# Routed experts' weights in a fused decoder kernel: one transfer of two chunks as 128 runs of 8 KB instead of 256 runs of 4 KB

## The reference

```python
def swiglu(x, w1, w3, w2):
    return (jax.nn.silu(x @ w1) * (x @ w3)) @ w2

def moe(h, w_router, router_bias, w1, w3, w2, ws1, ws3, ws2):   # E = 64, D = 1024, F = 256
    t = h.reshape(-1, D)                                        # 512 tokens
    scores = jax.nn.sigmoid((t @ w_router).astype(jnp.float32))
    _, eidx = lax.top_k(scores + router_bias.astype(jnp.float32), TOP_K_EXPERTS)
    ...
    def expert_block(args):                                     # 128 rows of one expert
        e, toks, gs = args
        xb = t[toks]
        return swiglu(xb, w1[e], w3[e], w2[e]) * gs[:, None]
    out = lax.map(expert_block, ...)
    routed = jax.ops.segment_sum(out.reshape(rows, D), row_tok, num_segments=n_tok)
    shared = swiglu(t, ws1, ws3, ws2)
    return (routed + shared).reshape(B, S, D)
```

## Time and profile before

| | us |
|---|---|
| median of 3 runs | 2543.27 |
| lowest and highest | 2539.15, 2545.02 |
| the profiled execution | 2526.87 |
| its span, first to last instruction | 2525.1 |

### The profile page before, as it was taken

One profiled execution on the slowest core, in us unless ns is written; L12 is line 12 of the kernel. 1 busy time (PEld: TensorE's weight loads), 2 busy tenths in 40 slices (PEclk: granted clock), 3 DMA queues, 4 the chain that ended last, 5 costly groups with the idle time before them and its releaser, 6 DMA issues.

```text
span 2525.1 us, 31999 instructions
## 1 busy us (share of the span) xinstructions
PE 2293.0 (91%) x10228; PEld 1778.9 (70%) x10228; DVE 1562.7 (62%) x2400; ACT 1195.4 (47%) x1778; POOL 283.9 (11%) x345
## 2 busy tenths in 40 slices
PE   6998999599999999994598989999989888999997
PEld 4776677487777777773475778887768556888875
DVE  6789654698888888886674553333453566433334
ACT  4432433298888888884235332233231673322322
POOL 0000002423223322324200000000000000000000
PEclk8999997799999999998699999999999989999999
DMA  7521132599999999996420222223313101232232
GB/s 305 200 95 64 42 130 94 150 357 380 371 365 368 372 355 357 359 339 238 175 93 8 67 75 100 91 100 100 100 67 100 34 1 67 100 100 93 99 101 83
DMA packets 124602, 422.63 MB, mean 167 GB/s; under 512 B 21024, under 2 KB 21152, under 8 KB 124384
## 3 DMA queue, kind: packets, MB, share of 16 engines
q1 hardware_dynamic: 98176, 367.86, 41.1%
q0 software_dynamic: 25376, 50.66, 5.3%
q10 hardware_dynamic: 960, 2.97, 0.3%
HBM read 419.68 MB, written 39.47 MB: 182 GB/s over the span
## 4 chain that ended last, share of the span: by engine, by line
PE 60%; DMA 16%; DVE 13%; issue 5%; ACT 4%; DVEq 1%; SPq 0%; POOL 0%; ACTq 0%; POOLq 0%
PE PS L283 17%; PE PS L285 17%; PE PS L284 17%; DMA eraw<-wstream 14%; DVE wl L191 3%; PE PS L628 3%; PE PS L650 2%; ACT wh L186 2%; DVE YA L2308 1%; PE PS L639 1%; DMA ada_w<-wada 1%; DVEq L1188 1%; ACT YS L1902 1%; DVE M L1185 1%; DVE X L555 1%
## 5 line engine op out<-in xcount | busy, mean ns | idle before, releaser
L191 DVE TENSOR_TENSOR wl<-raw,wh 128x1024 fp32r<-128x1024 f32 x239 | 292.5, 1225 | 403.3 <-ACT wh L186 396.9
L283 PE MATMUL PS<-HTh,wh 128*128 128x512 f32 x1248 | 503.8, 404 | 39.5 <-DVE HTl L581 18.7
L191 DVE TENSOR_TENSOR wl<-eraw,wh 128x1024 fp32r<-128x1024 f32 x384 | 460.1, 1225 | 73.5 <-ACT wh L186 72.9
L284 PE MATMUL PS<-HTl,wh 128*128 128x512 f32 x1248 | 492.0, 394 | 0.0
L285 PE MATMUL PS<-HTh,wl 128*128 128x512 f32 x1248 | 491.6, 394 | 0.0
L186 ACT ACTIVATE wh<-eraw 128x1024 fp32r<-128x1024 f32 x384 | 392.4, 1054 | 104.6 <-DMA eraw<-wstream 84.2
L186 ACT ACTIVATE wh<-raw 128x1024 fp32r<-128x1024 f32 x239 | 251.7, 1056 | 393.4 <-PE PS L285 371.6
L283 PEld LDWEIGHTS PS<-HTh,wh 128*128 128x128 f32 x1248 | 237.8, 191 | 105.3 <-issue 35.6
L284 PEld LDWEIGHTS PS<-HTl,wh 128*128 128x128 f32 x1248 | 238.2, 191 | 51.1 <-issue 3.4
L285 PEld LDWEIGHTS PS<-HTh,wl 128*128 128x128 f32 x1248 | 237.9, 191 | 51.2
L283 PE MATMUL PS<-wh,XTh 128*128 128x512 f32 x536 | 223.4, 417 | 5.0 <-DVE XTl L1873 2.4
(11 more groups left out here) (403 smaller groups left out, 3488.3 us busy)
## 6 DMA issues: line engine op xcount, KB each, us to landing
eraw<-wstream SPq DMA_DIRECT2D x192, 1024.0 KB, 15.6
raw<-wstream SPq DMA_DIRECT2D x240, 512.0 KB, 3.3
ada_w<-wada SPq DMA_DIRECT2D x24, 512.0 KB, 4.9
eraw<-wexp SPq DMA_DIRECT2D x9, 1024.0 KB, 9.4
ada_wb<-wada SPq DMA_DIRECT2D x2, 2048.0 KB, 16.0
ada_g<-wada SPq DMA_DIRECT2D x2, 2048.0 KB, 11.0
X<-xT SPq DMA_DIRECT2D x4, 512.0 KB, 8.1
ada_w<-wada SPq DMA_DIRECT2D x1, 2048.0 KB, 23.8
```

The source lines that it names most:

```text
L191: nc.vector.tensor_tensor(wl[:, ci % RING, :], src, wh[:, ci % RING, :].bitcast(F32), ALU.subtract).then_inc(split_done, 1)
L283: nc.tensor.matmul(o, lh, rh, start=start, stop=False)
L284: nc.tensor.matmul(o, lh, rl, start=False, stop=False)
```

## The change

The host lays out the 384 chunks of the routed experts differently. Of each pair of chunks that is fetched together, row p of the first chunk is followed directly by row p of the second. The bytes in `wstream` stay within the same 1 MB. The kernel's transfer now reads that 1 MB as 128 rows of 8 KB and writes 8 KB to each partition; the destination bytes are as before. The shape of the instruction goes from 128x2x1024 to 128x2048. No instruction is added, removed or moved on any engine, and no wait changes. The transfers into `raw`, those from `wexp`, and the gathers and scatters stay as they are.

```diff
         def expert_pair(j, ci):
 
-            return (eraw[:, ER_PLACE[j]:ER_PLACE[j] + 2, :], wstream[bass.ds(ci, 2)].rearrange("c p n -> p c n"))
+            return (eraw[:, ER_PLACE[j]:ER_PLACE[j] + 2, :].rearrange("p c n -> p (c n)"),
+                    wstream[bass.ds(ci, 2)].rearrange("c p n -> (c p n)").rearrange("(p n) -> p n", p=P))
@@ stream
     out += [np.zeros((P, CW), np.float32)] * (CHUNKS - len(out))
-    return np.stack(out)
+    w = np.stack(out)
+    pairs = w[EXPERT0:EXPERT1].reshape(3 * E, 2, P, CW)
+    w[EXPERT0:EXPERT1] = pairs.transpose(0, 2, 1, 3).reshape(6 * E, P, CW)
+    return w
```

## The result

The changed kernel takes 2525.03 us (median of 4 runs, 2523.97 to 2527.03) against 2543.41 us: ratio 0.9925, 95% interval [0.9913, 0.9936], 18.4 us less. Two later comparisons beside before gave 0.9946 [0.9932, 0.996] and 0.9925 [0.9896, 0.9953]. The forecast was 2521.

The account below looks back on a forecast made before the run. DMA engines bound the late routed-expert stage, PE the early part. 3 x 8 packets x 14 ns save 0.34 us an expert; 61 x 0.34 = 20.7 us off 2543.3 gives 2522.6, said as 2521; range 2502 to 2545.

Parts of the forecast that it names:

- The bound and the cap: Routed-expert stage: early experts at PE's 9.36 us, later 54 at the DMA engines' 10.08; faster transfers give at most 39 us.
- The 8 KB packet: Weight transfers of the routed experts: 313.1 ns against 327.2 for two of 4 KB, 14 ns less; near 341 with surplus.
- surplus: Expert-stage 4 KB row takes 177.8 ns, 14 more than 163.6; taken as a price per transfer, so the change keeps it.
- the sum: Expert stage: 3 transfers x 8 packets x 14 ns, 0.34 us less per expert and engine; 61 experts gain 20.7 us.
- near equality of 0.26 and 0.23 us: Surplus per transfer and engine, 0.26 us in the feed-forward stage, 0.23 in the expert stage; read as a transfer's price.
- the first rival: The rival "The surplus falls too" in the expert stage: 2504 us, chance 0.22; objection: feed-forward transfers start on idle engines.
- The period: DMA-bound part of the expert stage: time per expert goes from 10.08 to 9.74 us, still above PE's 9.36.
- The lead: Expert stage: full ring of 12 places lets PE keep its pace, 5.0 us in both kernels; 13 experts instead of seven.
- Bytes decide: Expert stage: memory, not the engines, limits it to 365 GB/s; no change, 2543 us, chance 0.14.
- The reads collide: Expert-stage weight reads: an 8 KB packet takes 378 ns, 0.54 us more per expert; 33 us slower, 2576, chance 0.11.
- The surplus falls too: Expert stage: extra 14 ns belong to packets; 8 KB takes 327 ns, gain stops at 39 us, 2504 us, chance 0.22.
- A small saving: Expert-stage packets: 4 ns saved instead of 14, 5.9 us in all, 2537 us; chance 0.11.

## Why the prediction was right, point by point

**The bound and the cap** were right. The late stretch is bound by the DMA engines, PE's pace is 9.36 us an expert, and half the bytes gave 570.96 us, 61 x 9.36, 40 us under before.

**The 8 KB packet.** Forecast 341 ns with its surplus; measured 338.6 ns in the first profile after (0.833 x 16 x 520 us, 167.10 MB) and 341.2 in the last. A pair of 4 KB packets took 358.6 (2 x 179.3), so a packet removed is worth 17 ns (14 to 19 from profile to profile), where the sum had 14. The working behind it was partly wrong, and that its result comes so near is in part luck. The fixed price is 9 ns by the medians, not 14; and the surplus is no price of a transfer. Doubling the transfers made the packets shorter (174.1 ns) and halving them left 179.6. It goes with bytes, 16 to 20 ns per 4 KB, and is a little smaller with 8 KB packets. The near equality of 0.26 and 0.23 us, on which I leaned, was chance: the feed-forward stage starts its transfers on idle engines, as the first rival had objected, and half the bytes bear it out. The same single-chunk transfers take 196.5 ns a packet there and 174.1 when the engines are full. The two errors pull apart: the fixed price was put too high, and the part of the surplus that the 8 KB packets save, some 8 ns a packet, was put at nothing. There the first rival was partly right.

**The period** in 640 to 1060 us (bytes of q1 over 3.146 MB an expert) was 10.12 and 10.14 us in the two profiles of before and 9.82, 9.79 and 9.80 in the three of the change: 0.30 to 0.35 less, against 0.34 forecast.

**The lead.** Forecast: 13 steps at PE's pace instead of 7; the traces have 14 instead of 9. The two steps more in before mean that the average of 10.08 us, taken from 569.28 on, was not yet the DMA engines' own period. With 10.12 us before's lead is 61 x 10.12 - 610.0 = 7.3 us, not 5.0; after it is 61 x 9.82 - 594.0 = 5.0. The sum took it to be the same in both kernels.

**The stage** took 594.0, 592.7 and 592.7 us against a forecast of 589.1: a gain of 16 to 19 us where the sum said 20.7. The length of the stage is off by the period, 9.74 in the sum and 9.80 measured, which starts from the 10.08 just named. The gain is off mainly by the lead, which shrank by some 2 us. Both misses are no larger than the 3 us between two executions of one kernel. Whole times fell by 18.4, 15.1 and 14.7 us.

**Rivals.** "Bytes decide" fell with the rows of 2 KB (+24 us). "The reads collide" fell for 8 KB rows: spacing 16 KB changes nothing. "The surplus falls too" would have meant 327 ns; the surplus for each 4 KB fell by a fifth, not by half. "A small saving" would have been 6 us. For this step the medians give 2.8% (318 against 309 ns) and the means 4.9%. The Trainium skill, "DMA: Bandwidth & Descriptors", section "Why small descriptors are slow (HBM only)", has about 3 cycles a packet, by which the prediction estimated 1.1%. The runs show more. The stage now moves 376 GB/s, gathers and scatters included. The same page of the Trainium skill, section "Where 436 GB/s comes from", lets the HBM side bind at about 358 GB/s; for this lone core the trace disagrees.

**Not foreseen:** the timed medians carry 20 us that go with the chip. They hardly touch the ratios, but I took the profiled execution's 16.4 us below the median for scatter.

## What to carry to other kernels

Where a stage has the DMA engines busy at 0.99, work out the mean time of a packet from share, stretch and count, and compare it with packets of another length in the same trace; a longer run is worth what the fixed part per packet says, here 3 to 5% of the transfer time for 8 KB against 4 KB, and no more at 16 KB. Keep all 128 partitions in each transfer, and watch the small transfers that share the engines: PE waited for them, and hardly for the weights, in the kernel with 16 KB rows. Compare profiles only when both start the stage at the same time, or compare the stage alone.

## What the runs showed of the hardware that was not expected

- 64 partitions at a time cut the transfer rate to 0.59: 220 against 375 GB/s, 583 against 341 ns for 8 KB.
- A packet's typical time is a fixed 9 ns and 150 ns for each 4 KB, from 2 to 16 KB (medians 84, 159, 309, 611 ns). The surplus of the mean sits in a few packets: 6% of the 4 KB ones, 319 ns more each.
- With 4 KB rows, single-chunk transfers of adjacent rows take 174.1 ns a packet (0.9976 of before's time), and with rows 8 KB apart 1.004 of it. With 8 KB rows no such difference shows (0.9944 against 0.9925, with intervals that overlap).
- Executions differ by 20 us in the shared expert of this program, and it goes with the chip: experts from 486 to 490 us and 2524 us for before, or from 506 to 513 us and 2544. In the late executions PE's longest wait near 450 us is 20.7 to 23.5 us. On ACT the first late instruction is the shared expert's `SGs`: 456.90 us in the first profile after, 446.48 in before. What holds it there stayed open; no experiment was made on it.
- With 16 KB rows the granted clock fell to 1.2 GHz in eight short stretches, the one shown after a wait of PE for a gather.
